# Token-by-token index projections against one pass over both tokens, with the head weights' product turned round

## The reference, cut to what matters

```python
proj = x @ w_in
q, k, v, qi, ki, wi = jnp.split(proj, DSA_SPLITS, axis=-1)   # qi 8 x 32 wide, ki 32, wi 8
...
rel = jax.nn.relu(jnp.einsum('bqhd,bsd->bqsh', qi_b, ki).astype(jnp.float32))
score = jnp.einsum('bqsh,bqh->bqs', rel, wi_b.astype(jnp.float32)) * idx_scale
score = jnp.where(causal, score, -jnp.inf)
_, idx = lax.top_k(score, topk)
...
x = layer_norm(ALPHA * x + h, ln_mix_g[i], ln_mix_b[i])
x = layer_norm(ALPHA * x + sq_relu_mlp(x, mlp_w1[i], mlp_w2[i]), ln_ffn_g[i], ln_ffn_b[i])
```

## Time and profile before

| | |
|---|---|
| runs | 1597.95, 1596.03, 1598.98 us; median 1597.95 |
| the profiled execution | 1597.95 us, its span 1596.1 us |
| PE busy | 1506.4 us, 94% of the span |
| DVE, ACT, POOL busy | 49%, 45%, 18% |
| mean granted TensorE clock | 0.973 of full speed |

### The profile page before, as it was taken

One profiled execution on the slowest core, in us unless ns is written; L12 is line 12 of the kernel. 1 busy time (PEld: TensorE's weight loads), 2 busy tenths in 40 slices (PEclk: granted clock), 3 DMA queues, 4 the chain that ended last, 5 costly groups with the idle time before them and its releaser, 6 DMA issues.

```text
span 1596.1 us, 20974 instructions
## 1 busy us (share of the span) xinstructions
PE 1506.4 (94%) x8668; PEld 1268.2 (79%) x8668; DVE 784.6 (49%) x995; ACT 714.0 (45%) x897; POOL 293.6 (18%) x111
## 2 busy tenths in 40 slices
PE   5999999999998999999999989998999999989998
PEld 4787748998875778748899868677999888879887
DVE  5325344444444344335454549965545456564445
ACT  3463433545434554334454436653544415354542
POOL 5685340000006594240000000000000003000000
PEclk8999999999998999999999999998999999989999
DMA  9531242545446441244554554114645443055542
GB/s 351 200 135 53 105 153 111 213 183 201 169 161 221 159 158 56 91 147 154 191 210 164 205 138 147 61 55 151 235 167 203 155 166 133 26 186 210 201 169 79
DMA packets 123009, 250.37 MB, mean 157 GB/s; under 512 B 16944, under 2 KB 28832, under 8 KB 122784
## 3 DMA queue, kind: packets, MB, share of 16 engines
q1 hardware_dynamic: 122912, 248.99, 44.1%
HBM read 247.93 MB, written 1.05 MB: 156 GB/s over the span
## 4 chain that ended last, share of the span: by engine, by line
PE 68%; issue 13%; POOL 10%; DVE 7%; ACT 1%; DMA 0%; SPq 0%; DVEq 0%; POOLq 0%; ACTq 0%
PE psum L448 67%; POOL w_lo L928 7%; POOL tmp L1388 2%; DVE x L2203 2%; PE psum L457 1%; DVE ht_hi L1097 1%; DVE ht_lo L1091 1%; DVE hT L1091 1%; DVE tiny L2254 1%; POOL big L1392 0%; DVE hT L2206 0%; DMA work<-in_cmp_pos_v 0%; DVE ht_lo L2197 0%; DVE w_lo L928 0%; POOL big L1391 0%
## 5 line engine op out<-in xcount | busy, mean ns | idle before, releaser
L448 PE MATMUL psum<-ht_hi,w_lo 128*128 128x256 f32 x1024 | 290.9, 284 | 4.1 <-DVE ht_lo L1091 2.8
L448 PE MATMUL psum<-w_lo,ht_hi 128*128 128x512 f32 (+1 forms) x544 | 215.3, 396 | 0.0
L448 PE MATMUL psum<-w_lo,hid_hi 128*128 128x512 f32 x512 | 202.4, 395 | 0.0
L448 PEld LDWEIGHTS psum<-ht_hi,w_lo 128*128 128x128 f32 x1024 | 195.4, 191 | 6.7 <-DVE ht_lo L1091 3.2
L908 ACT ACTIVATE w_hi_work<-ring 128x2048 fp32r<-128x2048 f32 (+1 forms) x47 | 88.3, 1879 | 178.7 <-PE psum L448 161.3
L928 DVE TENSOR_TENSOR w_lo<-ring,w_hi_work 128x2048 fp32r<-128x2048 f32 x30 | 68.8, 2292 | 135.4 <-ACT w_hi_work L908 135.4
L928 POOL TENSOR_TENSOR w_lo<-ring,w_hi_work 128x2048 fp32r<-128x2048 f32 (+1 forms) x17 | 76.0, 4472 | 305.7 <-ACT w_hi_work L908 305.7
L961 DVE TENSOR_TENSOR hid_lo<-work,hid_hi 128x512 fp32r<-128x512 f32 x64 | 44.2, 691 | 174.3 <-ACT hid_hi L950 174.3
L448 PE MATMUL psum<-ht_lo,w_hi_rows 128*128 128x256 f32 x448 | 125.0, 279 | 0.0
L448 PE MATMUL psum<-ht_lo,w_hi_tmp 128*128 128x256 f32 x448 | 125.0, 279 | 0.0
L448 PE MATMUL psum<-ht_hi,w_hi_tmp 128*128 128x256 f32 x448 | 124.8, 279 | 0.0
(11 more groups left out here) (354 smaller groups left out, 3377.4 us busy)
## 6 DMA issues: line engine op xcount, KB each, us to landing
ring<-in_w_ff SPq DMA_DIRECT2D x32, 2048.0 KB, 8.8
ring<-in_mlp_w SPq DMA_DIRECT2D x32, 2048.0 KB, 8.5
ring<-in_w_in SPq DMA_DIRECT2D x20, 2048.0 KB, 8.0
ring<-in_w_out SPq DMA_DIRECT2D x4, 2048.0 KB, 8.0
ring<-in_w_ple_gate SPq DMA_DIRECT2D x4, 2048.0 KB, 7.9
ring<-in_sb_ssm_w_in SPq DMA_DIRECT2D x4, 2048.0 KB, 13.8
ring<-in_dsa_w_in SPq DMA_DIRECT2D x3, 2048.0 KB, 8.4
ring<-in_w_up_nsa SPq DMA_DIRECT2D x2, 2048.0 KB, 7.9
```

Source lines behind the costliest of these rows:

```text
L448: ins = pe.matmul(o, lhsT, rhs, start=start, stop=stop)
```

## The change

The names `qi` and `kiw` change places in the order of the PSUM banks. PE turns token 1 first, waits for all four `x_turned`, and then makes each product once for both tokens: qi with 256 columns (`units_by_tile`), ki as 32 rows with 256 columns, and wi with the operands exchanged: `hT` is loaded and the eight columns of wi stream, so that it comes out with tokens on partitions, in columns 256 to 271 of the bank that also holds ki. The turn of wi, its table `wiT` and three signals go away. ACT copies qi first, then, when ki and wi are both done, places ki four times and copies wi, scaled. The first index matmuls wait for that last copy.

```diff
--- before.py
+++ after.py
@@ -136,7 +136,7 @@
 
 WIDE2 = ["sq0", "sq1", "kk", "sk0", "kk2", "sk1", "sv0", "sv1", "sA", "sB"]
 WIDE2 += ["glu0", "glu1"] + _mlp_names("A.", FB // 2, "f")
-WIDE2 += ["kiw", "qi", "dk", "dv", "dq0", "dq1", "dq2", "dq3", "do0", "do1", "dt0"]
+WIDE2 += ["qi", "kiw", "dk", "dv", "dq0", "dq1", "dq2", "dq3", "do0", "do1", "dt0"]
 WIDE2 += ["do2", "dt1", "do3", "dt2", "do4", "dt3", "do5", "dt4", "dt5"] + _mlp_names("B.", FB // 2, "f")
 AUX2 = _mlp_names("A.", 4, "x") + ["ct0", "ct1"] + [f"bu{q}" for q in range(4)] + [f"cs{h}" for h in range(8)]
 AUX2 += ["y0", "y1"]
@@ -1447,7 +1447,6 @@
     relu_ = part(5120, 2048)
     isc, irep = part(7168, 384), part(7552, 384)
     iadd = irep
-    wiT = isc[:, 0:S]
     m8 = tiny[:, 470:478]
     wi = tiny[:, 480:496]
     dob = big[:, 0:2048].rearrange("p (t n) -> p t n", t=TT)
@@ -1469,8 +1468,7 @@
     y_placed_dve, y_placed_act, y_ready = sig("y_placed_dve"), sig("y_placed_act"), sig("y_ready")
     ln_stats, ln_done = sig("ln_stats"), sig("ln_done")
     idx_ready, idx_relu, idx_summed = sig("idx_ready"), sig("idx_relu"), sig("idx_summed")
-    kiz_zero, kiz_ready = sig("kiz_zero"), sig("kiz_ready")
-    wi_rows, wi_turned = sig("wi_rows"), sig("wi_turned")
+    kiz_zero = sig("kiz_zero")
     dsc_ready, dsc_read, dmax_ready, dexp_ready, masked = (sig(n) for n in (
         "dsc_ready", "dsc_read", "dmax_ready", "dexp_ready", "masked"))
     dpt_ready, dpt_saved_dve, dpt_saved_act, dhigh_ready, dso_ready = (sig(n) for n in (
@@ -1764,33 +1762,23 @@
         turn(1, 0)
         turn(1, 1)
         kit.mlp("A.", 0, lambda: turn(2, 0))
+        turn(2, 1)
+        pe.wait_ge(x_turned.sem, st.at(x_turned, 4))
         w = next_tile("ds3", KT, DSA_IN - I_QI)
-        kiw, nth = wide_.next("kiw")
+        kit.units_by_tile(wide_, ["qi"], w)
+        b, nth = wide_.next("kiw")
         pe.wait_ge(wide_.saved.sem, st.at(wide_.saved, nth))
-        b, nth = wide_.next("qi")
-        pe.wait_ge(wide_.saved.sem, st.at(wide_.saved, nth))
+        for k in range(KT):
+            mm(b[0:32, 0:S], w[:, k, I_KI - I_QI:I_WI - I_QI], hT[:, k, :], k == 0, k == KT - 1)
         for t in range(TT):
-            if t:
-                turn(2, 1)
-            pe.wait_ge(x_turned.sem, st.at(x_turned, 2 * t + 2))
-            tok = slice(t * P, (t + 1) * P)
             for k in range(KT):
-                mm(kiw[0:40, tok], w[:, k, I_KI - I_QI:DSA_IN - I_QI], hT[:, k, tok], k == 0, k == KT - 1,
-                   wide_.ready if t == 1 and k == KT - 1 else None)
-            for u in range(2):
-                for k in range(KT):
-                    mm(b[:, u * S + t * P:u * S + (t + 1) * P], w[:, k, u * P:(u + 1) * P], hT[:, k, tok],
-                       k == 0, k == KT - 1, wide_.ready if t == u == 1 and k == KT - 1 else None)
+                mm(b[:, S + 8 * t:S + 8 * t + 8], hT[:, k, t * P:(t + 1) * P], w[:, k, I_WI - I_QI:DSA_IN - I_QI],
+                   k == 0, k == KT - 1, wide_.ready if t == 1 and k == KT - 1 else None)
         tile_done()
-        pe.wait_ge(wi_rows.sem, st.at(wi_rows, 1))
-        for t in range(TT):
-            mm(bank[2][:, 8 * t:8 * t + 8], wiT[32:40, t * P:(t + 1) * P], ident[32:40, 32:40], True, True,
-               wi_turned if t else None)
 
         def index_scores(t):
             if t == 0:
-                pe.wait_ge(kiz_ready.sem, st.at(kiz_ready, 1))
-                pe.wait_ge(wide_.saved.sem, st.at(wide_.saved, wide_.nth_save("qi")))
+                pe.wait_ge(wide_.saved.sem, st.at(wide_.saved, wide_.nth_save("kiw")))
             else:
                 pe.wait_ge(idx_relu.sem, st.at(idx_relu, 1))
             keys = (t + 1) * P
@@ -2101,19 +2089,14 @@
         for t in range(TT):
             ln_deviation(2, t)
 
+        save("qi", flat(qiT))
         b, nth = wide_.next("kiw")
         act.wait_ge(wide_.ready.sem, st.at(wide_.ready, nth))
-        act.activation(wiT[32:40, :], b[32:40, 0:S], ACT.Copy, scale=IDX_DIM ** -0.5 * IDX_HEADS ** -0.5) \
-            .then_inc(st.up(wi_rows), 1)
         act.wait_ge(kiz_zero.sem, st.at(kiz_zero, 1))
         for hl in range(4):
-            act.activation(kiz[32 * hl:32 * hl + 32, hl, :], b[0:32, 0:S], ACT.Copy) \
-                .then_inc(st.up(kiz_ready if hl == 3 else act_step), 1)
-        q, nth = wide_.next("qi")
-        act.wait_ge(wide_.ready.sem, st.at(wide_.ready, nth))
-        act.wait_ge(wi_turned.sem, st.at(wi_turned, 1))
-        act.activation(wi, bank[2][:, 0:16], ACT.Copy).then_inc(st.up(wide_.saved), 1)
-        act.activation(flat(qiT), q, ACT.Copy).then_inc(st.up(wide_.saved), 1)
+            act.activation(kiz[32 * hl:32 * hl + 32, hl, :], b[0:32, 0:S], ACT.Copy).then_inc(st.up(act_step), 1)
+        act.activation(wi, b[:, S:S + 16], ACT.Copy, scale=IDX_DIM ** -0.5 * IDX_HEADS ** -0.5) \
+            .then_inc(st.up(wide_.saved), 1)
 
         def index_relu(t):
             act.wait_ge(idx_ready.sem, st.at(idx_ready, t + 1))
```

## The result

The changed kernel took 1613.74 us in the median of 4 runs (1613.43 to 1616.67), the kernel before 1597.04 (4 runs beside them): a ratio of 1.0115, 95% interval 1.0100 to 1.0131, or 16.7 us slower. Slower was forecast (0.97), but at 1609.5 and with 1613.0 as the upper end. Six further runs of the changed kernel, without the kernel before beside them, took 1614.34 to 1618.62 us; the profiled one is among them. The direction and the stage were right; the price was too low: 11.5 us were forecast, 16.7 came.

The account below looks back on a forecast made before the run. The prediction took TensorE (PE) as the bound, busy 94% of the span. It added 7.5 us of structure and 4.0 us of clock falls, +11.5, to 1597.95 us: 1609.5 us, range 1604 to 1613.

Parts of the forecast that it names:

- PE sets the end, and nothing behind the hand-over swallows a delay: From the first index matmul on, PE has no slack (busy 35.56 of 35.60 us), so any delay is paid.
- Rival (d): PE slack behind the first index matmul swallows the lost 11.4 us, leaving only savings: 1594.8 us, chance 0.03.
- The structure, +7.5: Wait for both tokens, products and ACT's copies put the first index matmul at 1307.92 against 1300.44, without clock effects.
- Token 1 is ready: Turned right after layer norm, token 1 is ready for PE at 1291.54, 1.74 us earlier than 1293.28.
- The products: PE's wi with exchanged operands: 32 eight-column instructions at 119 ns each, 3.80 us.
- ACT's wait: PE stands bare for 1.97 us before the first index matmul while ACT copies ki four times, then wi.
- Rival (c): Eight-column wi products cost half, 1.9 us: 1607.6 us with the clock falls, 1603.6 without; chance 0.09.
- The 62 ns: Skill page's issue gap for narrow matmuls, by which wi would take 2.0 us; the forecast followed the trace instead.
- Two falls of the clock: PE's clock drops from 2.4 to 1.2 GHz at layer norm's hole and at the wi products with ACT's wait.
- Rival (a): The clock stays up in one or both holes: 1607.5 us with one fall, 1605.5 with none; chance 0.17.
- The size of a low stretch, 2.0 us each: Each of two clock falls on PE costs 2.0 us, together 4.0; bounds nothing and 3.5 each.
- rival (b): The low clock stretches are long, 3.5 us each, and wi's products slow at 175 ns (+1.8): 1614.3 us, chance 0.09.

Follow-up runs that it names:

- e10_spread: e1_warm with the sixteen wi products spread, one ahead of each qi product, and ki last: 1606.71 us, ratio to the kernel before 1.0053.
- e1_warm: The changed kernel with six unread 512-column filler products in PE's layer norm hole: 1610.84 us, ratio to the kernel before 1.0066.
- e3_merged: The kernel before with only the merging: token 1 turned first, ki with wi and qi in 256 columns, wi still turned: 1606.56 us, ratio 1.0044.
- e6_fill: e1_warm with two more 512-column fillers between the last wi product and the first index matmul: 1609.51 us, ratio to the kernel before 1.0076.
- e9_order_warm: The changed kernel with ki and wi first, qi last, and e1_warm's fillers in layer norm's hole: 1607.80 us, ratio to the kernel before 1.0049.
- e7_swap: The kernel before with ACT's last two copies exchanged, qi ahead of the turned wi, index matmuls waiting for qi alone: 1598.04 us, ratio 1.0004.
- e4_wi_only: The kernel before with only wi's operands exchanged, token by token, ki and wi ahead of qi: 1600.91 us, ratio 1.0004.
- e8_warm_norms: e7_swap with filler products in PE's holes of the two layer norms ahead of MLPs: 1594.08 us, ratio to the kernel before 0.9977.

## Why the prediction was wrong, point by point

*PE sets the end, and nothing behind the hand-over swallows a delay.* Right. From B to C every kernel whose clock is 1.00 there takes 36.49 us to the hundredth, early or late. Rival (d) is out.

*The structure, +7.5.* Right: 7.43 in e10_spread. The parts too. Token 1 is ready 1.68 us earlier (8.01 us behind A in e1_warm, 9.69 in before), where I had 1.74. The merging costs 3.2, if its low stretch costs the 3.50 that e1_warm shows for the first one (6.70 less 3.50 in e3_merged). The products: 3.6 us for 32 at 112 ns, where I took 119; ACT's wait 1.95, where I had 1.97. Rival (c), cheap narrow products, is out. The 62 ns that the Trainium skill gives in "TensorE: Matmul & The Clock Gate", section "Back-to-back issue gap", are for the gap of a matmul without its weight load; with a load at each the runs show 112.

*Two falls of the clock.* Right in place and number. Rival (a) is out.

*The size of a low stretch, 2.0 us each.* This step failed. The first cost 3.50 (after against e1_warm, A to C), the second 4.02 (e1_warm, +11.45, less the 7.43 of the structure): 7.5 together, where I put 4.0. I had sized them by two holes of before whose low stretch ended within 3.4 us. The hole that is most like the new one, a layer norm with PE waiting and transposes at its end, was in the same rows as evidence for rival (b): the clock still at 0.50 from 1104 to 1106. And the narrow products behind 114.6, which I took as a sign of the second fall, were not followed to their end. These two low stretches of before last about 10 us, with PE busy for most of them (columns as in the earlier trace rows):

```profile
117.20:127.00 9.80, 8.18 (x37) 7.01 (x38) 6.69 (x9) 2.22 (x2) 9.80 (x9) 0.50 0.52 198
1097.00:1106.80 9.80, 7.31 (x33) 6.94 (x34) 8.43 (x9) 4.90 (x5) 0.00 (x0) 0.50 0.68 271
```

In after both low stretches are of that kind (1292.0 to 1302.2 and 1312.5 to 1322.7). My upper bound of 3.5 each is what the first measured, and too low for the second. Rival (b) was the nearest, for a reason that is only partly its own: the eight-column products bring the clock down (e6_fill, e9_order_warm), but wi was never slowed throughout, as it assumed; the products took 4.75 us, not 5.6.

*The rest.* Structure and clock make 14.95 us between A and C; the medians differ by 16.7, with an interval from 16.0 to 20.9. So 1.1 us or more lie outside of the stage, 1.7 by the medians. Behind C the profiles scatter by 1.5 us, and ahead of A there is no difference in the code; what the remainder is stays open. Of the 5.2 us by which the forecast of the difference missed, the clock is 3.5 and the remainder 1.7. That the time came within 0.6 us of rival (b)'s 1614.3 is partly luck: its two low stretches at 3.5 are near the measured 7.5, but its 1.8 for slow products stands where the remainder is.

## What to carry to other kernels

Here work that stood in another engine's wait was worth more than its own time, because it also kept the clock up: taking token 0's products out of layer norm's shadow cost 3.2 us of cover and 3.5 of clock. When a hole is opened in TensorE's work, size the low clock by the trace's own hole of the same kind, followed to its end, not by the shortest one. A product with the operands exchanged, to get its result the other way round, was no cheaper for its eight columns: 112 ns for an instruction, as with 32 columns. Sixteen such products took 3.6 us, where the turn of the finished result by two 8x8 matmuls and the copies behind it took 1.5, and 0.84 with the qi copy beside it (e7_swap). If it must be, spread them among wide ones: that saved 2.4 us (e10_spread against e1_warm).

## What the runs showed of the hardware

A busy TensorE can lose its clock. In e6_fill and e9_order_warm PE had no hole ahead of it, but a run of 32 instructions of eight columns (3.6 us at full clock) brought the granted clock from 1.00 to 0.50 in its course, which cost 3.3 us in e9_order_warm, most of it in the wide products behind. The same 32, spread among products of 256 columns, left it at 1.00 (e10_spread), and so did two runs of 16 (e4_wi_only). Each of these is one profiled execution, and whether the few columns count or the share of the weight loads wasn't told apart. And the low clock outlasts the return to work: in after PE's products with 256 columns ran from 1296.47, and the clock came back only at 1302.2; in e3_merged from 1294.32 to about 1299.7. Products that nobody reads, put in the hole, keep it up: the two holes filled in e8_warm_norms gave 4.0 us together. A wait need not be long: behind ACT's 1.95 us in e10_spread, with the clock at 1.00 and 256-column products up to the wait, it fell for 3.4 us (1309.7 to 1313.1).
